# Second-half rows added by the transfer itself: five reads moved from SyncE to GpSimd, tiles finished in the order 3, 0, 2, 1, 4

## The chip, the cores and the metric

The kernel runs on one core of a Trainium2 chip. The metric is the device time of one execution in microseconds (us). Before the change three runs took 617.83, 620.12 and 621.11 us.

## What is computed

The reference is one layer of a flow-matching backbone for 512 latent and 128 context tokens of width 1024: modulation, normalization, attention beside a recurrent block, an output projection with a gated residual, and then a mixture of experts. The change touches only the last line of it, where the experts' output is added to the residual:

```python
x = x + g1 * (jnp.concatenate([attn, rec], axis=-1) @ lp['w_out'])      # x1 of the kernel
h2 = modulate(rms_norm(x, lp['norm2']), sh2, sc2)
x = x + g2 * moe(h2, ...)      # top 1 of 4 groups, then top 2 of its 8 experts
```

Each token has two experts, so each output row is x1 plus two expert rows (already multiplied by g2 and by the expert's weight).

## The kernel before

The 640 tokens are five tiles of 128 rows: tiles 0 to 3 are latent, tile 4 is context. The mixture of experts runs in steps: each takes a pair of experts with up to 64 token slots each, gathers their rows (GpSimd, line 863), multiplies by the weights (TensorE, lines 1821 and 1839), and VectorE (line 1383) evicts the 128 result rows into `y`. GpSimd scatters them to `y_rows` in HBM (line 879), which has 1280 rows: 640 for a token's first expert and 640 for its second. `y_rows` is filled with zeros by ten transfers of GpSimd much earlier (line 842). The rows of the last step are not scattered at all; TensorE multiplies them by a 0/1 matrix `chosen`, which puts each row where its token is, and leaves the result in PSUM. A token's first-half row from the step before the last is sent to the second half, so that the first half can be read one scatter earlier.

The end of the kernel then has, for each tile, four terms: the first-half rows, the second-half rows, x1, and the `chosen` product.

- **SyncE (SP)** waits until all but the last scatter have landed, then issues the loads of the first-half rows into `yk` (line 521: tiles 3, 4, 0, 1, 2) and of the x1 rows of tiles 2, 0 and 1 that had been spilled (line 518, into `x1b`). It then waits for the last scatter (the wait at line 531 ends with it) and issues five loads of the second-half rows into the buffer `y1` (line 533). After that it waits for each finished tile in the order 0 to 4 and issues its store (line 536; tile 4 in two halves, line 540).
- **GpSimd (POOL)** adds x1 to tiles 3 and 4 (line 890), and then the second-half rows to tile 4 (line 893).
- **VectorE (DVE)** adds x1 to tiles 0 and 1 (`base`, line 1395), the first before the eviction of the last step (line 1426), the second after it. It adds the second-half rows to tiles 0, 1 and 2 (`with_late`, line 1402), and to every tile its PSUM sums (`finish`, line 1408; `finish_last` in two halves, line 1416).
- **TensorE (PE)** brings x1 of tile 2 into PSUM with two products by the identity (line 1874), then computes the `chosen` products of the tiles in the order 0 to 4 (line 1889). For tile 3 it also adds the second-half rows by identity products (`PE_SUMS`, line 1887). Tile 4 uses the PSUM bank of tile 0 and waits until that is finished.

Everything in this order is written out by hand with semaphores; `rows_in[t]` counts the transfers that fill tile t (16 each), `y1_in[t]` the second-half transfer, `y_out` the scatters, `fin` the finished tiles. The core of the loop over tiles on VectorE is:

```python
for t in range(3):
    with_late(t)
    finish(t)
dve.wait_ge(S["base"], 1)
finish(3)
dve.wait_ge(S["base"], NT - SPILLED + 1)
finish_last()
```

Of the kernel before, what the change touches and what calls it, by code (L numbers as in the profile page):

```python
# [16 lines left out]
P = 128  # L17
# [7 lines left out]
SPILLED = LT - 1  # L25
PE_SUMS = (3,)
PE_BASE = SPILLED - 1
# [53 lines left out]
def build(nc, a):  # L81

    with ExitStack() as ctx:
# [105 lines left out]
        def temp(c, lo, n):  # L189
# [44 lines left out]
        yk = rf[:, 0:NT * D].rearrange("p (t n) -> p t n", t=NT)  # L234
        y1 = rf[:, NT * D:2 * NT * D].rearrange("p (t n) -> p t n", t=NT)
        x1b = ring[:, HOME[5], 0:SPILLED * D].rearrange("p (t n) -> p t n", t=SPILLED)
# [10 lines left out]
            "out_done v p act xg_in xt_mm gu_mm dn_mm xT_v xT_a th_ok act_ok aT_mm aT_ok y_v idxc_ok pidc_ok y_out "  # L247
            "y_zero gu_half x1b_in base stepw w_mm now gsel chosen tail_mm fin sg_ok turn cache_out st_col st_t st_ev").split()}
        rows_in = [sem(f"rows_in{i}") for i in range(NT)]
# [85 lines left out]
        def tail_bank(t):  # L335

            return (0, 4, 2, 6, 0)[t]

# [27 lines left out]
        def _(sp):  # L366
# [155 lines left out]
            for t in range(SPILLED, NT):  # L522
                first_half(t)
            x1_back(PE_BASE, S["x1b_in"])
            for t in range(PE_BASE):
                x1_back(t, rows_in[t])
                first_half(t)
            first_half(PE_BASE)
            steps = sp.value_load(last[0:1, PAIRS - 1:PAIRS])
            sp.wait_ge(S["y_out"], 16 * steps)  # L530
            sp.sem_inc(S["turn"], 1)
            for t in range(NT):
                sp.dma_start(y1[:, t, :], a["y_rows"][TOK + t * P:TOK + (t + 1) * P, :]).then_inc(y1_in[t], 16)
            for t in range(NT - 1):
                sp.wait_ge(S["fin"], t + 1)
                sp.dma_start(y_dst[t], yk[:, t, :]).then_inc(S["out_done"], 16)
# [267 lines left out]
        def _(pool):  # L804
# [82 lines left out]
            for t in range(SPILLED, NT):  # L887
                pool.wait_ge(rows_in[t], 32)
                row = yk[:, t, :].rearrange("p (c n) -> p c n", c=DC)
                pool.tensor_tensor(row, row, x1_row(t), ALU.add).then_inc(S["base"], 1)  # L890
            pool.wait_ge(S["base"], NT - SPILLED)
            pool.wait_ge(y1_in[NT - 1], 16)
            pool.tensor_tensor(yk[:, NT - 1, :], yk[:, NT - 1, :], y1[:, NT - 1, :], ALU.add).then_inc(S["base"], 1)


        @block.vector
        def _(dve):
# [494 lines left out]
            def base(t):  # L1392

                dve.wait_ge(rows_in[t], 48)
                step(dve.tensor_tensor(yk[:, t, :], yk[:, t, :], x1b[:, t, :], ALU.add))

            def with_late(t):

                if t == PE_BASE:
                    dve.wait_ge(rows_in[t], 32)  # L1400
                dve.wait_ge(y1_in[t], 16)
                step(dve.tensor_tensor(yk[:, t, :], yk[:, t, :], y1[:, t, :], ALU.add))

            def finish(t):

                dve.wait_ge(S["tail_mm"], t + 1)
                b = tail_bank(t)
                dve.tensor_tensor(yk[:, t, :], yk[:, t, :], wide[:, b * 512:b * 512 + D], ALU.add)\
                   .then_inc(S["fin"], 1)
            def finish_last():  # L1410

                b = tail_bank(NT - 1)
                for half in range(2):
                    dve.wait_ge(S["tail_mm"], NT + half)
                    cols = slice(half * 512, (half + 1) * 512)
                    dve.tensor_tensor(yk[:, NT - 1, cols], yk[:, NT - 1, cols], ps[:, b + half, :], ALU.add)\
                       .then_inc(S["fin"], 1)
# [17 lines left out]
            base(1)  # L1435
            for t in range(3):
                with_late(t)
                finish(t)
            dve.wait_ge(S["base"], 1)
            finish(3)  # L1440
            dve.wait_ge(S["base"], NT - SPILLED + 1)
            finish_last()


        @block.tensor
        def _(pe):
# [424 lines left out]
            pe.wait_ge(S["act_ok"], steps * FC + FC)  # L1871
            pe.wait_ge(S["x1b_in"], 16)
            for half in range(2):
# [3 lines left out]
            pe.wait_ge(S["xT_a"], steps + 1)  # L1877
            for t in range(NT):
                if t >= 4:
                    pe.wait_ge(S["fin"], t - 3)  # L1880
                if t in PE_SUMS:
                    pe.wait_ge(y1_in[t], 16)
                for half in range(2):
                    if t == 0:
                        pe.wait_ge(S["y_v"], steps + 1 + half)
                    if t in PE_SUMS:
                        pe.matmul(ps[:, tail_bank(t) + half, :], ident[:, :], y1[:, t, half * 512:(half + 1) * 512],
                                  start=True, stop=False)
                    ins = pe.matmul(ps[:, tail_bank(t) + half, :], chosen[:, t, :],
                                    y[:, half * 512:(half + 1) * 512], start=t not in PE_SUMS and t != PE_BASE, stop=True)  # L1890
                    if half or t == NT - 1:
                        ins.then_inc(S["tail_mm"], 1)
# [60 lines left out]
```

## Time and profile before

| what | us |
|---|---|
| three runs | 617.83, 620.12, 621.11 |
| the profiled execution, own time | 619.67 |
| its span, first to last instruction | 617.8 |
| TensorE busy | 589.3 |
| VectorE busy | 346.2 |
| ScalarE busy | 179.7 |
| GpSimd busy | 102.2 |
| mean granted clock of TensorE, share of full | 0.989 |

The profile is that of one execution. A busy time is the sum of an engine's instructions; a wait is idle time of an engine before an instruction, with what released it. The chain of waits follows the work that ended last back through its releasers. Times in the rows count from the start of the span.

### The profile page before, as it was taken

Reading aid. Unit: us, or ns where it says so; the run is one execution under the profiler, and the core shown is the slowest. Engines: PE = TensorE matmul, PEld = TensorE weight load, DVE = VectorE, ACT = ScalarE, POOL = GpSimd, SP = SyncE. Lnnn points to the kernel's source line nnn. Section 1 sums busy time; section 2 is a strip of 40 time slices with the busy share of each in tenths; the row PEclk is TensorE's granted clock in tenths of the full one; section 3 lists DMA queues with packets and bytes.
Section 4 is the critical chain, followed back from the end, with each engine's and each line's share of the span. In section 5 each row is a group of like instructions: output and inputs, shape, how many; then the busy total and the mean of one; then the engine's idle time right before and its main releaser. Section 6 shows DMA issues by size and latency. Waiting matters only on the chain.

```text
span 617.8 us, 9369 instructions
## 1 busy us (share of the span) xinstructions
PE 589.3 (95%) x3276; PEld 327.9 (53%) x3277; DVE 346.2 (56%) x780; ACT 179.7 (29%) x375; POOL 102.2 (17%) x134
## 2 busy tenths in 40 slices
PE   5989999999998999999999989999999999997997
PEld 2544455455565667645554536555555555554552
DVE  2745898755565888664666784333433343432347
ACT  4203787701145787731111101111111111110110
POOL 4000011121233000000000101212121212121241
PEclk9999999999999999999999889999999999997999
DMA  8999833530028728629113879999999999999997
GB/s 319 375 369 362 321 143 145 188 136 2 1 71 251 301 83 237 285 93 415 71 69 119 310 269 336 415 418 418 420 417 420 417 419 420 419 418 418 419 382 301
DMA packets 47922, 175.95 MB, mean 285 GB/s; under 512 B 11556, under 2 KB 17712, under 8 KB 34320
## 3 DMA queue, kind: packets, MB, share of 16 engines
q1 hardware_dynamic: 36240, 154.60, 64.2%
q0 software_dynamic: 6688, 15.48, 7.2%
q10 hardware_dynamic: 4960, 5.42, 2.5%
q8 instruction: 21, 0.34, 0.2%
q14 instruction: 13, 0.11, 0.0%
HBM read 163.11 MB, written 21.14 MB: 298 GB/s over the span
## 4 chain that ended last, share of the span: by engine, by line
PE 78%; DMA 14%; SPq 4%; DVE 2%; ACTq 1%; issue 1%; ACT 0%; DVEq 0%; POOLq 0%
PE ps L1821 19%; PE ps L1634 11%; PE ps L1839 9%; PE ps L1559 8%; PE ps L1547 7%; DMA expert_w<-exp_w_up 5%; PE ps L1674 4%; PE ps L1701 4%; DMA gate_w<-lru_wx 3%; PE ps L1683 3%; PE ps L1787 2%; DMA w_mod_ring<-w_mod 2%; SPq L374 2%; PE ps L1522 2%; PE ps L1468 2%; DMA recurrence<-w_mod 2%
## 5 line engine op out<-in xcount | busy, mean ns | idle before, releaser
L1821 PE MATMUL ps<-expert_w,hT_mixT 128*64 128x256 f32 x1120 | 136.0, 392 | 6.1 <-DMA expert_w<-exp_w_up 5.7
L1821 PEld LDWEIGHTS ps<-expert_w,hT_mixT 128*64 128x64 f32 x1120 | 84.7, 136 | 61.2 <-issue 17.8
L1547 PE MATMUL ps<-hT_mixT,w 128*128 128x128 f32 (+1 forms) x256 | 72.6, 437 | 1.2 <-DVE hT_mixT L970 1.2
L1634 PE MATMUL ps<-w,hT_mixT 128*128 128x512 f32 x160 | 71.9, 597 | 0.0
L1839 PE MATMUL ps<-expert_w,hT_mixT 128*64 128x512 f32 x276 | 65.8, 598 | 0.0
L786 ACT ACTIVATE hT_mixT<-ps 128x128 f32<-128x128 f32 x36 | 10.0, 278 | 187.1 <-PE ps L1821 187.1
L1547 PEld LDWEIGHTS ps<-hT_mixT,w 128*128 128x128 f32 x256 | 38.9, 191 | 35.8 <-issue 32.6
L1365 DVE SCALAR_TENSOR_TENSOR hT_mixT<-hT_mixT,ps 128x128 f32<-128x128 f32 x36 | 10.4, 288 | 79.8 <-ACT hT_mixT L786 79.8
L1559 PE MATMUL ps<-w_qkv,hT_mixT 128*128 128x512 f32 (+1 forms) x160 | 53.1, 488 | 0.0
L1383 DVE TENSOR_TENSOR w<-ps,w 128x1024 f32<-128x1024 f32 x17 | 20.8, 1225 | 56.6 <-PE ps L1839 56.6
L1634 PEld LDWEIGHTS ps<-w,hT_mixT 128*128 128x128 f32 x160 | 29.1, 191 | 29.9 <-issue 29.7
L1559 PEld LDWEIGHTS ps<-w_qkv,hT_mixT 128*128 128x128 f32 x160 | 29.8, 190 | 21.6 <-issue 19.7
L1839 PEld LDWEIGHTS ps<-expert_w,hT_mixT 128*64 128x64 f32 x276 | 19.0, 136 | 32.3 <-issue 30.3
L1132 DVE TENSOR_REDUCE softmax_stat<-ps 128x1 f32<-128x640 f32 (+1 forms) x40 | 28.6, 715 | 10.3 <-PE ps L1674 10.2
L1674 PE MATMUL ps<-k_stack,q_stack 128*128 128x320 f32 (+1 forms) x144 | 30.6, 331 | 3.3 <-ACT q_work L716 3.3
L879 POOL DMA_INDIRECT y_rows<-w,slot_row_now x17 | 24.0, 1412 | 58.1 <-DVE w L1383 58.1
L1674 PEld LDWEIGHTS ps<-k_stack,q_stack 128*128 128x128 f32 x144 | 21.3, 188 | 16.8 <-issue 11.5
L716 ACT ACTIVATE q_work<-ps,softmax_stat 128x640 f32<-128x640 f32 (+1 forms) x40 | 28.3, 708 | 4.4 <-DVE softmax_stat L1133 3.9
L711 ACT ACTIVATE w_qkv<-ps 128x640 f32<-128x640 f32 (+1 forms) x40 | 24.7, 619 | 14.5 <-PE ps L1683 14.2
L863 POOL DMA_INDIRECT w<-h_rows,slot_token_now x17 | 17.6, 1036 | 66.9 <-PE ps L1787 62.3
L1701 PE MATMUL ps<-w_qkv,v_tok 128*64 128x256 f32 x168 | 25.6, 400 | 0.0
L1683 PE MATMUL ps<-ident,q_work 128*128 128x128 f32 x168 | 25.2, 275 | 0.0
(297 smaller groups left out, 765.5 us busy)
## 6 DMA issues: line engine op xcount, KB each, us to landing
expert_w<-exp_w_down SPq DMA_DIRECT2D x30, 1024.0 KB, 17.5
expert_w<-exp_w_gate SPq DMA_DIRECT2D x29, 1024.0 KB
expert_w<-exp_w_up SPq DMA_DIRECT2D x29, 1024.0 KB
w_mod_ring<-w_mod SPq DMA_DIRECT2D x14, 1024.0 KB, 6.5
y_rows<-zero_rows POOLq DMA_DIRECT2D x10, 512.0 KB, 6.0
expert_w<-y_rows SPq DMA_DIRECT2D x10, 512.0 KB, 7.9
recurrence<-w_mod SPq DMA_DIRECT2D x8, 512.0 KB, 9.8
w<-w_in SPq DMA_DIRECT2D x4, 1024.0 KB, 16.8
```

The lines of the kernel that those rows point to most:

```text
L711: act.activation(probT[:, m % HEADS, 0:k], wide[:, 4 * 512:4 * 512 + k], ACT.Copy).then_inc(S["pT_a"], 1)
L716: act.activation(probs(n), scores(n), ACT.Exp, scale=SCALE, bias=sm[:, 1, n:n + 1], accum_out=sm[:, 2, n:n + 1]).then_inc(S["prob"], 1)
L879: pool.indirect_dma_start(a["y_rows"], bass.IndirectOffsetOnAxis(pidc[:, 0:1], 0), y, None, bounds_check=TOP * TOK - 1, oob_is_err=False). ...
L1132: step(dve.tensor_reduce(sm[:, 0, n:n + 1], scores(n), AXY, ALU.max))
L1547: ins = pe.matmul(ps[:, bank, 0:n], w1v[:, c, m * P:(m + 1) * P], HM[:, c, lo:lo + n], start=(c == 0), stop=(c == DC - 1))
L1559: ins = pe.matmul(ps[:, bank, 0:n], HM[:, c, t * P:(t + 1) * P], wqv[:, c, lo:lo + n], start=(c == 0), stop=(c == DC - 1))
L1634: ins = pe.matmul(ps[:, 2 * (t % 2) + half, :], HM[:, c, t * P:(t + 1) * P], w1v[:, c, half * 512:(half + 1) * 512], start=(c == 0), stop= ...
L1674: ins = pe.matmul(ps[:, bank, 0:k], qs[:, h, t * P:(t + 1) * P], ks[:, g, s, lo:lo + k], start=(s == 0), stop=(s == 1))
L1683: ins = pe.transpose(ps[:, 4 + i // 4, (i % 4) * P:(i % 4 + 1) * P], prob[:, m % 3, i * P:(i + 1) * P], ident[:, :])
L1701: ins = pe.matmul(out.rearrange("p (b n) -> p b n", b=2), vt[:, i if t < LT else NT, g * HD:(g + 1) * HD], probT[:, 4 * g + e:4 * g + 4:2, ...
L1821: ins = pe.matmul(ps[r, 2 + k, 0:2 * P].rearrange("p (k f) -> p k f", k=2), xT[:, c, r], gate_up(i)[:, :, c, k:FF:FC], start=(c == 0), sto ...
L1839: ins = pe.matmul(ps[r, 5 + half, :].rearrange("p (a n) -> p a n", a=4), actT[:, c, r], down(i, c, half), start=(c == 0), stop=(c == FC - 1))
```

## The change

The second-half rows are no longer loaded into a buffer `y1` by SyncE. GpSimd issues five transfers from `y_rows` straight onto `yk` with `accum_op=ALU.add`, so that the transfer adds what it reads to what is there. Each may start only when its tile's first-half rows (and the x1 add, where VectorE or GpSimd makes one) are in `yk`: GpSimd waits for its own two adds, for the last scatter, and between the transfers for VectorE's adds (a new semaphore `own_base`) and for the first-half rows of tile 2. It issues them in the order 3, 0, 4, 2, 1. The adds of the second-half rows on VectorE (three tiles), on GpSimd (tile 4) and on TensorE (tile 3) are gone. TensorE, VectorE and the stores take the tiles in the order 3, 0, 2, 1, 4, with other PSUM banks for them. SyncE goes from its first-half loads straight to the waits for finished tiles.

```diff
--- before.py
+++ after.py
@@ -23,7 +23,7 @@
 NT = TOK // P
 LT = LAT // P
 SPILLED = LT - 1
-PE_SUMS = (3,)
+TAIL = (3, 0, 2, 1, 4)
 PE_BASE = SPILLED - 1
 HEADS, KV, HD = 8, 2, 64
 QK = HEADS + KV
@@ -232,7 +232,6 @@
         th, sg, act2, actT = (HM[:, FC * i:FC * (i + 1), P:2 * P] for i in range(4))
         rf = ring[:, 1:3, :].rearrange("p r n -> p (r n)")
         yk = rf[:, 0:NT * D].rearrange("p (t n) -> p t n", t=NT)
-        y1 = rf[:, NT * D:2 * NT * D].rearrange("p (t n) -> p t n", t=NT)
         x1b = ring[:, HOME[5], 0:SPILLED * D].rearrange("p (t n) -> p t n", t=SPILLED)
         numbers = zero[:, :]
 
@@ -245,7 +244,7 @@
             "mod2_in bc_ok shift_in g2_in route_in prepared bias_mm "
             "pair_ok rank_mm rank_rd slot idx_mm tid_ok gexp_in gexp route_ok "
             "out_done v p act xg_in xt_mm gu_mm dn_mm xT_v xT_a th_ok act_ok aT_mm aT_ok y_v idxc_ok pidc_ok y_out "
-            "y_zero gu_half x1b_in base stepw w_mm now gsel chosen tail_mm fin sg_ok turn cache_out st_col st_t st_ev").split()}
+            "y_zero gu_half base own_base stepw w_mm now gsel chosen tail_mm fin sg_ok turn cache_out st_col st_t st_ev").split()}
         rows_in = [sem(f"rows_in{i}") for i in range(NT)]
         w1_in = [sem(f"w1_in{i}") for i in range(LC)]
         h2_at = [sem(f"h2_at{i}") for i in range(2)]
@@ -334,7 +333,7 @@
 
         def tail_bank(t):
 
-            return (0, 4, 2, 6, 0)[t]
+            return (4, 6, 2, 0, 0)[t]
 
         def at_expert(src, x):
             return src[x] if isinstance(x, int) else src[bass.ds(x, 1)]
@@ -521,18 +520,13 @@
                 sp.dma_start(yk[:, t, :], a["y_rows"][t * P:(t + 1) * P, :]).then_inc(rows_in[t], 16)
             for t in range(SPILLED, NT):
                 first_half(t)
-            x1_back(PE_BASE, S["x1b_in"])
+            x1_back(PE_BASE, x1_at)
             for t in range(PE_BASE):
                 x1_back(t, rows_in[t])
                 first_half(t)
             first_half(PE_BASE)
-            steps = sp.value_load(last[0:1, PAIRS - 1:PAIRS])
-            sp.wait_ge(S["y_out"], 16 * steps)
-            sp.sem_inc(S["turn"], 1)
-            for t in range(NT):
-                sp.dma_start(y1[:, t, :], a["y_rows"][TOK + t * P:TOK + (t + 1) * P, :]).then_inc(y1_in[t], 16)
-            for t in range(NT - 1):
-                sp.wait_ge(S["fin"], t + 1)
+            for i, t in enumerate(TAIL[:-1]):
+                sp.wait_ge(S["fin"], i + 1)
                 sp.dma_start(y_dst[t], yk[:, t, :]).then_inc(S["out_done"], 16)
             for half in range(2):
                 sp.wait_ge(S["fin"], NT + half)
@@ -888,9 +882,19 @@
                 pool.wait_ge(rows_in[t], 32)
                 row = yk[:, t, :].rearrange("p (c n) -> p c n", c=DC)
                 pool.tensor_tensor(row, row, x1_row(t), ALU.add).then_inc(S["base"], 1)
+            def second_half(t):
+                pool.dma_start(yk[:, t, :], a["y_rows"][TOK + t * P:TOK + (t + 1) * P, :], accum_op=ALU.add).then_inc(y1_in[t], 16)
             pool.wait_ge(S["base"], NT - SPILLED)
-            pool.wait_ge(y1_in[NT - 1], 16)
-            pool.tensor_tensor(yk[:, NT - 1, :], yk[:, NT - 1, :], y1[:, NT - 1, :], ALU.add).then_inc(S["base"], 1)
+            pool.wait_ge(S["y_out"], 16 * (end + 1))
+            pool.sem_inc(S["turn"], 1)
+            second_half(3)
+            pool.wait_ge(S["own_base"], 1)
+            second_half(0)
+            second_half(4)
+            pool.wait_ge(rows_in[PE_BASE], 32)
+            second_half(2)
+            pool.wait_ge(S["own_base"], 2)
+            second_half(1)
 
 
         @block.vector
@@ -1392,24 +1396,19 @@
             def base(t):
 
                 dve.wait_ge(rows_in[t], 48)
-                step(dve.tensor_tensor(yk[:, t, :], yk[:, t, :], x1b[:, t, :], ALU.add))
-
-            def with_late(t):
-
-                if t == PE_BASE:
-                    dve.wait_ge(rows_in[t], 32)
+                dve.tensor_tensor(yk[:, t, :], yk[:, t, :], x1b[:, t, :], ALU.add).then_inc(S["own_base"], 1)
+
+            def finish(i, t):
+
                 dve.wait_ge(y1_in[t], 16)
-                step(dve.tensor_tensor(yk[:, t, :], yk[:, t, :], y1[:, t, :], ALU.add))
-
-            def finish(t):
-
-                dve.wait_ge(S["tail_mm"], t + 1)
+                dve.wait_ge(S["tail_mm"], i + 1)
                 b = tail_bank(t)
                 dve.tensor_tensor(yk[:, t, :], yk[:, t, :], wide[:, b * 512:b * 512 + D], ALU.add)\
                    .then_inc(S["fin"], 1)
             def finish_last():
 
                 b = tail_bank(NT - 1)
+                dve.wait_ge(y1_in[NT - 1], 16)
                 for half in range(2):
                     dve.wait_ge(S["tail_mm"], NT + half)
                     cols = slice(half * 512, (half + 1) * 512)
@@ -1433,12 +1432,8 @@
             base(0)
             last_y_evict(end)
             base(1)
-            for t in range(3):
-                with_late(t)
-                finish(t)
-            dve.wait_ge(S["base"], 1)
-            finish(3)
-            dve.wait_ge(S["base"], NT - SPILLED + 1)
+            for i, t in enumerate(TAIL[:-1]):
+                finish(i, t)
             finish_last()
 
 
@@ -1869,25 +1864,20 @@
                 visits(q, q % HELD, 1 + q // HELD, kept=q == PAIRS - 2, kept_half=q == KEPT_HALF)
             steps = pe.value_load(last[0:1, PAIRS - 1:PAIRS])
             pe.wait_ge(S["act_ok"], steps * FC + FC)
-            pe.wait_ge(S["x1b_in"], 16)
+            pe.wait_ge(x1_at, 16 * (SPILLED + 1))
             for half in range(2):
                 pe.matmul(ps[:, tail_bank(PE_BASE) + half, :], ident[:, :], x1b[:, PE_BASE, half * 512:(half + 1) * 512],
                           start=True, stop=False)
             pe.wait_ge(S["chosen"], NT)
             pe.wait_ge(S["xT_a"], steps + 1)
-            for t in range(NT):
-                if t >= 4:
-                    pe.wait_ge(S["fin"], t - 3)
-                if t in PE_SUMS:
-                    pe.wait_ge(y1_in[t], 16)
+            for i, t in enumerate(TAIL):
+                if i == NT - 1:
+                    pe.wait_ge(S["fin"], 1)
                 for half in range(2):
-                    if t == 0:
+                    if i == 0:
                         pe.wait_ge(S["y_v"], steps + 1 + half)
-                    if t in PE_SUMS:
-                        pe.matmul(ps[:, tail_bank(t) + half, :], ident[:, :], y1[:, t, half * 512:(half + 1) * 512],
-                                  start=True, stop=False)
                     ins = pe.matmul(ps[:, tail_bank(t) + half, :], chosen[:, t, :],
-                                    y[:, half * 512:(half + 1) * 512], start=t not in PE_SUMS and t != PE_BASE, stop=True)
+                                    y[:, half * 512:(half + 1) * 512], start=t != PE_BASE, stop=True)
                     if half or t == NT - 1:
                         ins.then_inc(S["tail_mm"], 1)
```

## Rows read from the trace of the kernel before

**Rows 1.** The page: busy time by engine; shares of the chain by engine.

```profile
PE 589.3 (95%) x3276; PEld 327.9 (53%) x3277; DVE 346.2 (56%) x780; ACT 179.7 (29%) x375; POOL 102.2 (17%) x134
...
PE 78%; DMA 14%; SPq 4%; DVE 2%; ACTq 1%; issue 1%; ACT 0%; DVEq 0%; POOLq 0%
```

**Rows 2.** Chain of waits, 590 to 618 us: start us, us, what.

```profile
601.24 1.91 PE ps L1874 x4
603.15 5.15 PE ps L1889 x12
608.30 1.12 PE ps L1887 x2
609.42 0.86 PE ps L1889 x2
610.28 0.86 PE ps L1887 x2
611.14 0.87 PE ps L1889 x2
```

**Rows 3.** Instructions of VectorE in order of time, 590 to 618 us: start us, us.

```profile
599.09 1.23 DVE L1395 TENSOR_TENSOR expert_w<-expert_w 128x1024 f32<-128x1024 f32 x1 [1.82 <-DMA expert_w<-y_rows]
...
602.72 1.22 DVE L1395 TENSOR_TENSOR expert_w<-expert_w 128x1024 f32<-128x1024 f32 x1
604.24 1.23 DVE L1402 TENSOR_TENSOR expert_w<-expert_w 128x1024 f32<-128x1024 f32 x1 [0.30 <-DMA expert_w<-y_rows]
605.50 1.22 DVE L1408 TENSOR_TENSOR expert_w<-expert_w,ps 128x1024 f32<-128x1024 f32 x1
...
610.28 1.22 DVE L1408 TENSOR_TENSOR expert_w<-expert_w,ps 128x1024 f32<-128x1024 f32 x1
612.11 1.22 DVE L1408 TENSOR_TENSOR expert_w<-expert_w,ps 128x1024 f32<-128x1024 f32 x1 [0.61 <-PE ps L1889]
613.25 1.28 DVE L1416 TENSOR_TENSOR expert_w<-expert_w,ps 128x512 f32<-128x512 f32 x2
```

**Rows 4.** Issues on SP's queue in order of time, 560 to 618 us.

```profile
587.45 0.80 SPq L521 DMA_DIRECT2D expert_w<-y_rows  x2
...
590.99 0.94 SPq L521 DMA_DIRECT2D expert_w<-y_rows  x2
599.09 2.29 SPq L533 DMA_DIRECT2D expert_w<-y_rows  x5
606.75 6.94 SPq L536 DMA_DIRECT2D y_sample<-expert_w  x4
```

**Rows 5.** Instructions of GpSimd in order of time, 560 to 618 us.

```profile
595.86 2.38 POOL L890 TENSOR_TENSOR expert_w<-expert_w,x_tok 128x1024 f32<-128x1024 f32 x1
609.65 2.81 POOL L893 TENSOR_TENSOR expert_w<-expert_w 128x1024 f32<-128x1024 f32 x1 [11.42 <-DMA expert_w<-y_rows]
```

**Rows 6.** Windows of 2 us: last columns are TensorE's clock, DMA busy share, GB/s.

```profile
599.00:601.00 2.00, 2.00 (x12) 0.50 (x8) 1.23 (x1) 0.00 (x0) 0.00 (x0) 1.00 1.02 393
...
605.00:607.00 2.00, 2.00 (x6) 0.91 (x5) 1.97 (x3) 0.00 (x0) 0.00 (x0) 1.00 1.06 418
```

**Rows 7.** DMA by queue, 599 to 609.6 us: packets, MB, share.

```profile
q1 hardware_dynamic: 1048, 3.79, 92.2%
```

**Rows 8.** Zero-filling transfers issued by GpSimd (line 842), and their order of time.

```profile
L842 POOL DMA_DIRECT2D y_rows<-zero_rows x10: 847/976/1167, 180.1 to 211.2; - x10
...
DMA to landing us min/median/max: 3.9/6.0/11.8
...
188.41 2.60 POOL L842 DMA_DIRECT2D y_rows<-zero_rows  x3 [5.61 <-issue]
197.12 2.81 POOL L842 DMA_DIRECT2D y_rows<-zero_rows  x3 [6.11 <-issue]
211.18 1.00 POOL L842 DMA_DIRECT2D y_rows<-zero_rows  x1 [11.25 <-issue]
```

**Rows 9.** The first-half loads (line 521): issue to landing.

```profile
DMA to landing us min/median/max: 5.9/10.2/11.4
```

## The prediction

> **What bounds the kernel now.** I went from the page to the end of the kernel. The page shows TensorE busy for 95% of the span and on the chain of waits for most of it [rows 1]; but the change leaves the expert loop alone and touches only what follows the last expert step, so the question is which wait ends last between about 599 us and the end. The chain of waits there [rows 2] is TensorE's: the identity products that put the x1 rows of tile 2 into PSUM, then the `chosen` products of tiles 0, 1 and 2 without a gap (5.15 us, 1.72 a tile), then tile 3, which needs 3.7 us as it also adds its second-half rows by two identity products (1.12 and 0.86), then tile 4. VectorE adds tile 3, then the two halves of tile 4, and the queue stores them. VectorE itself [rows 3] is the second chain: from 604.24 it is full with three pairs of adds of 1.22 us and ends them at 611.50, 0.6 us before TensorE lets it go on with tile 3. Its last add ends at 613.25 + 1.28 = 614.53; 3.3 us later the span of 617.8 ends.
>
> The third party is the transfers. The first-half rows and the x1 rows go out on SP's queue from 587.45 on, and after the last scatter but one has landed (599.09) the five second-half loads follow within 2.3 us [rows 4]. They land late and one by one: VectorE gets tile 0 at 604.24 [rows 3], TensorE waits for tile 3 until 608.30 [rows 2], GpSimd for tile 4 until 609.65 [rows 5]. From the first to the fifth that is 5.4 us, 1.35 us a tile of 512 KB, about 390 GB/s, and the windows show why: the 16 DMA engines are full until 607, at 393 GB/s in the first window and 418 in the last [rows 6]. Until 609.6 SP's queue moved 3.79 MB [rows 7]; less five loads (2.62) and the store of tile 0 (0.52), 0.65 MB were still left of the first-half rows at 599.1, 1.7 us of work. So the landings follow a simple sum: 599.1 + 1.7 + 2.0 (issue and landing) + 1.35 for each tile, which gives 604.15 for the first and 609.55 for the fifth, against 604.24 and 609.65 in the trace.
>
> **Part by part.** *Removed from VectorE:* three adds of second-half rows, 3 x 1.22 = 3.7 us [rows 3]. *From TensorE:* two identity products for tile 3 (1.12 + 0.86) and the wait in front of them; five tiles then take 5 x 1.72 from 603.15, that is until 611.7, where they now end at 613.7. *From GpSimd:* the add of tile 4, 2.81 us [rows 5], which ends at 612.5 and is covered by TensorE now. *From SP:* the wait for the scatter and five issues (2.29 us), which nothing else was waiting behind: its stores start at 606.75.
>
> *With the transfers free of charge* the end would go by TensorE and VectorE: four adds end at 610.0 + 0.1 + 1.22 = 611.4, the halves of tile 4 at about 612.6, 1.9 us before 614.53. That is the most this change can gain, 0.3% of the run. A measurement of this kernel tells about 0.5% (3.1 us) from no change.
>
> *Moved to GpSimd:* five transfers. GpSimd is done with its two base adds at 598.24 [rows 5], before the scatter lands at 599.09, so moving that wait costs nothing. An issue on GpSimd takes 0.98 us where SP takes 0.46, 2.29 for five [rows 4, 8]: the first transfer starts 0.5 us later, the others wait in the DMA queue in any case. The order is tile 3 (599.1), the wait for VectorE's base add of tile 0 (ends 600.3 [rows 3]), tiles 0 and 4 (until 602.3), the wait for the first-half rows of tile 2, tile 2 (about 603.3), and the wait for VectorE's base add of tile 1, which runs behind the last eviction and ends at 603.94; tile 1 is issued until 604.9. Behind each wait stand all later transfers, and VectorE's finishing adds wait for them. The first-half rows of tile 2 were issued last, at about 591.5; such loads land 5.9 to 11.4 us after issue [rows 9], so by 602.9 at the latest. With the engines busy on the earlier tiles, none of these waits empties the queue.
>
> *The unknown price* is that of a transfer that adds; no row shows one. For each 512 KB it has to read the row in HBM and also the row that is in `yk`, and to write once. Call s the time of one tile. Not under 1.35, since it reads all that the plain load reads and the engines are full with those; the nearest row for moving both operands is two plain transfers, 2 x 1.35 = 2.7. With reads, reads and write one after another it would be three, 4.05. I take 2.7: the windows show 1.0 busy share at the rate of one read and one write [rows 6], so nothing is free there for a second read. The Trainium skill, "Collectives: The Full Stack", section "The bandwidth ceiling", says that a reducing step runs at about half the rate of a copying one, since both operands are read through the same ring; no run of before shows it, and by it the sum would be the one below. The Trainium skill, "DMA: Bandwidth & Descriptors", section "Anatomy of one DMA", gives for a transfer from GpSimd 2.0 us plus its bytes at 436 GB/s and no surcharge for an add, 1.2 us a tile as an estimate; by it the change would come out as the first rival.
>
> **The sum.** Landings, from 599.1 + 1.7 + 2.0 = 602.8: tile 3 at 605.5, tile 0 at 608.2, tile 4 at 610.9, tile 2 at 613.6, tile 1 at 616.3. VectorE: tile 3 605.6 to 606.8, tile 0 608.3 to 609.5, then it idles until 613.7, tile 2 until 614.9, tile 1 616.4 to 617.6, the halves of tile 4 until 618.9. Against 614.53 that is +4.4 us. The last stores leave with the same spacing as now, so the 3.3 us behind them stay. In general the end moves by 5s - 9.1 us, and never below -1.9: no change at s = 1.8, +0.5% at s = 2.45. The stores of tiles 3 and 0 now leave at 606.8 and 609.5, amid the transfers; at 1.35 each that is up to 2.7 more, +7.1 in all. Now the store of tile 0, issued at 606.75, runs amid the loads of tiles 3 and 4 without widening the 1.35, so I count nothing for it and keep +7.1 as the upper end. The profiled execution took 619.67 us, 1.9 around its span of 617.8, and with +4.4 would be 624.1; the median of the runs, 620.12, is 0.45 higher, and the forecast is for it: 624.5.
>
> **The rivals.** *Adding costs no more than loading (s = 1.35).* Tile 3 lands at 604.7 for the slower issue, tile 0 at 606.0, tile 4 at 607.4, tile 2 at 608.7, tile 1 at 610.1; VectorE ends tile 3 at 606.2, tile 0 at 607.9, tile 2 at 610.0, tile 1 at 611.4, the halves at 612.7: -1.8, 618.3 us. For it: the second operand is on the chip already, and only the read from HBM may count. Against it: full engines at one read per byte. It decides below s = 1.8. Chance 0.24.
> *In between (s from 1.7 to 2.4),* if the second read goes on in part beside the write: -0.6 to +2.9, at s = 2.0 +0.9, 621.0. Chance 0.17.
> *Room in GpSimd's queue.* The zero-filling transfers of the same size, also issued by GpSimd, went out three at a time, with 5.6, 6.1 and 11.3 us of idling in between which no instruction explains [rows 8]. If adding transfers need as much room, tiles 3, 0 and 4 go out until 602.3, then GpSimd stands 5.6 to 11.3 us; tile 1 is out at about 609.9 at the earliest and lands 3.9 later (the fastest landing there [rows 8]), 613.8; then adds of 1.3 and 1.28 until 616.4: +1.9, up to +7.6 with the long stall, even at s = 1.35. Against it: those transfers read their zeros in pieces of 512 bytes, these read whole rows of 4 KB. Chance 0.07, mostly slower.
> *Three times the cost (s = 4.05):* +11, 631. Chance 0.07.
> The forecast, s of about 2.5 to 3 with or without the stores' share (+3.3 to +7.1): chance 0.45; its own range is 623.4 to 627.2.
>
> **How the numbers follow.** Faster by over 0.5% is in none of these cases: 0.02 for what I have not seen. Within 0.5%: the cheap case less that 0.02, the one in between, and 0.02 of the queue's: 0.41. Slower: 0.45 + 0.05 + 0.07 = 0.57. The range runs from the cheap case, 618.0, to a little over the upper end with both stores, 628.0; the tripled cost and the long stall lie outside.
>
> **What would show it.** The time from the issue of an adding transfer to VectorE's finishing add, and the spacing of the finishes of tiles 0, 2 and 1: 5.4 and 2.7 us by the forecast, with VectorE waiting for GpSimd's transfers about 4 us before tile 2 and 1.5 before tile 1; by the cheap case it waits for TensorE and is never idle over 1 us. TensorE should end its products at 611.7 in either, and GpSimd issue five transfers between 599 and 605; a gap after the third is the queue's room. I am wrong if VectorE's last add ends before 617 with 2.7 a tile, or if the time before 599 us moves by over 1 us.

## The result, and the profile after

Seven runs of the changed kernel took 622.72 to 626.54 us, median 624.29; seven of the kernel before, taken beside them, took 617.83 to 621.11, median 619.60. The ratio is 1.0095 (5.9 us), 95% interval 1.0075 to 1.0114: slower by 4.6 to 7.1 us; the two medians are 4.7 apart. The profiled execution has a span of 623.4 us against 617.8.

The page of the changed kernel: span, busy times, and the chain's shares by engine (as in [rows 1]).

```profile
span 623.4 us, 9352 instructions
...
PE 585.7 (94%) x3272; PEld 326.4 (52%) x3273; DVE 343.2 (55%) x777; ACT 179.7 (29%) x375; POOL 103.2 (17%) x138
...
PE 73%; DMA 17%; SPq 4%; DVE 2%; issue 1%; ACTq 1%; ACT 0%; DVEq 0%; POOL 0%; POOLq 0%
```

TensorE has 3.6 us less to do, VectorE 3.0, and TensorE's share of the chain has gone from 78 to 73%, that of the transfers from 14 to 17. The chain of waits at the end (start, duration, what) says where, against [rows 2]:

```profile
589.82 12.38 DMA expert_w<-y_rows
...
603.04 14.70 DMA expert_w<-y_rows
...
617.76 0.04 DVE expert_w L1406
...
617.91 1.66 DVEq L83
619.58 0.60 DVE expert_w L1415
```

TensorE isn't in it any more. It runs from the first-half rows over GpSimd's last issue to 14.7 us of waiting for one transfer, the second-half rows of tile 1, and from there to VectorE. VectorE in order of time, against [rows 3]:

```profile
598.44 1.22 DVE L1399 TENSOR_TENSOR expert_w<-expert_w 128x1024 f32<-128x1024 f32 x1 [2.45 <-DMA expert_w<-y_rows]
...
601.38 1.21 DVE L1399 TENSOR_TENSOR expert_w<-expert_w 128x1024 f32<-128x1024 f32 x1
604.60 1.22 DVE L1406 TENSOR_TENSOR expert_w<-expert_w,ps 128x1024 f32<-128x1024 f32 x1 [2.01 <-DMA expert_w<-y_rows]
607.65 1.22 DVE L1406 TENSOR_TENSOR expert_w<-expert_w,ps 128x1024 f32<-128x1024 f32 x1 [1.84 <-DMA expert_w<-y_rows]
614.33 1.22 DVE L1406 TENSOR_TENSOR expert_w<-expert_w,ps 128x1024 f32<-128x1024 f32 x1 [5.45 <-DMA expert_w<-y_rows]
617.76 1.22 DVE L1406 TENSOR_TENSOR expert_w<-expert_w,ps 128x1024 f32<-128x1024 f32 x1 [2.21 <-DMA expert_w<-y_rows]
618.90 1.28 DVE L1415 TENSOR_TENSOR expert_w<-expert_w,ps 128x512 f32<-128x512 f32 x2
```

The four lines 1406 are the finishes of tiles 3, 0, 2 and 1. Before each VectorE sat idle until its adding transfer landed: 2.01, 1.84, 5.45 and 2.21 us. TensorE had ended its `chosen` products long before, at 601.71 + 8.75 = 610.46:

```profile
601.71 8.75 PE L1879 MATMUL ps<-w,hT_mixT 128*128 128x512 f32 x20
```

GpSimd (against [rows 5]) waits for the last scatter, for VectorE and for the first-half rows of tile 2, 2.1 us in all, and has issued everything by 604.24:

```profile
595.20 2.37 POOL L884 TENSOR_TENSOR expert_w<-expert_w,x_tok 128x1024 f32<-128x1024 f32 x1
598.45 1.00 POOL L886 DMA_DIRECT2D expert_w<-y_rows  x1 [0.88 <-DMA y_rows<-w,slot_row_now]
599.97 1.84 POOL L886 DMA_DIRECT2D expert_w<-y_rows  x2 [0.52 <-DVE expert_w L1399]
602.48 1.76 POOL L886 DMA_DIRECT2D expert_w<-y_rows  x2 [0.67 <-DMA expert_w<-y_rows]
```

The windows of the transfers in that time show full engines, as [rows 6], but half the bytes: 205 and 211 GB/s at a share over 1.0 (each added row is counted once). The stores join them late: the one of tile 3 is issued at 605.84, but SyncE's queue q1 moves nothing from 603 to 609 and 0.73 MB from 609 to 615, with the adding transfers (q0) beside it. The second fence gives the two queues for 609 to 615.

```profile
603.00:605.00 2.00, 2.00 (x6) 0.95 (x5) 0.40 (x1) 0.00 (x0) 1.24 (x2) 1.00 1.07 205
...
607.00:609.00 2.00, 2.00 (x6) 0.81 (x5) 1.22 (x1) 0.00 (x0) 0.00 (x0) 1.00 1.07 211
...
611.00:613.00 2.00, 0.00 (x0) 0.00 (x0) 0.00 (x0) 0.00 (x0) 0.00 (x0) 1.00 1.05 281
```

```profile
q0 software_dynamic: 234, 0.88, 73.8%
q1 hardware_dynamic: 195, 0.73, 32.4%
```

The queues from 598 to 618 us (packets, MB, share of 16 engines) price it: GpSimd's queue, q0, moved its five tiles with 69.0% of 20 us, 2.76 us a tile. This share runs a little high for adding transfers, since their packets overlap (the share of the windows above is 1.07).

```profile
q0 software_dynamic: 720, 2.62, 69.0%
q1 hardware_dynamic: 655, 2.36, 29.9%
```

Counted from TensorE's first `chosen` product (602.99 before, 601.71 after), VectorE's last add ends after 11.5 us before and after 18.5 us now; the expert loop ended 1.3 us earlier in this profiled execution, so the span shows 5.6 of the 6.9.

### The profile page after: what moved, and what is told of

It reads as the page before. It is cut to its first block, busy times and chain, and to the rows that moved or that the text cites. A ratio compares the mean times of both kernels' runs of the same rounds, so it can differ in the third digit from the quotient of the medians.

```text
span 623.4 us, 9352 instructions
## 1 busy us (share of the span) xinstructions
PE 585.7 (94%) x3272; PEld 326.4 (52%) x3273; DVE 343.2 (55%) x777; ACT 179.7 (29%) x375; POOL 103.2 (17%) x138
## 4 chain that ended last, share of the span: by engine, by line
PE 73%; DMA 17%; SPq 4%; DVE 2%; issue 1%; ACTq 1%; ACT 0%; DVEq 0%; POOL 0%; POOLq 0%
PE ps L1816 17%; PE ps L1629 11%; PE ps L1542 8%; PE ps L1554 8%; PE ps L1834 7%; DMA expert_w<-exp_w_up 5%; DMA expert_w<-y_rows 4%; PE ps L1669 4%; PE ps L1696 4%; DMA gate_w<-lru_wx 3%; PE ps L1517 3%; PE ps L1678 3%; SPq L373 2%; PE ps L1463 2%; PE ps L1782 2%; DMA recurrence<-w_mod 2%
## 5 line engine op out<-in xcount | busy, mean ns | idle before, releaser
L1387 DVE TENSOR_TENSOR w<-ps,w 128x1024 f32<-128x1024 f32 x17 | 20.8, 1224 | 56.5 <-PE ps L1834 56.5
L1669 PEld LDWEIGHTS ps<-k_stack,q_stack 128*128 128x128 f32 x144 | 21.3, 188 | 17.2 <-issue 11.5
```

Source lines behind the costliest of these rows:

```text
L1669: ins = pe.matmul(ps[:, bank, 0:k], qs[:, h, t * P:(t + 1) * P], ks[:, g, s, lo:lo + k], start=(s == 0), stop=(s == 1))
```

## Experiments

All runs below start from one of the two kernels. They also bound each step number that an engine loads, with two register instructions per load; a control with that alone was not run. Kernels with and without the adding have it alike. The time behind "beside" is the median of the kernel before in the same rounds, and the ratio has its 95% interval in brackets. In what follows "first issue" is the issue of the first second-half transfer, 599.09 in the kernel before and 598.45 in the changed one, where the last add ends 21.7 us later (15.4 in the kernel before). What released that issue differs between the runs, so the count from TensorE's first `chosen` product (18.5 and 11.5 us) stands beside it where the two disagree.

**Plain transfers in the same places.**

```diff
-pool.dma_start(yk[:, t, :], ..., accum_op=ALU.add).then_inc(y1_in[t], 16)
+pool.dma_start(yk[:, t, :], ...).then_inc(y1_in[t], 16)
```

> The changed kernel with the adding taken off its five transfers: GpSimd issues the same reads at the same places, onto the same rows, but they overwrite what is there (so the first-half rows and the x1 added to them are left out of the output). As in all runs that follow, the step numbers that the engines load are bounded by two more register instructions each; that is before the stage in question, so times of the stage are counted from the landing of the last scatter. Theory (an adding transfer takes 2.6 to 2.7 us of the full engines where a plain one takes 1.35): the five take 1.35 each, VectorE's last add ends some 5 to 7 us earlier than in the changed kernel, counted from the landing of the last scatter; the time is 618 to 619.5 us, 0 to 2 below the kernel before. Rival 1 (issuing from GpSimd, or its waits, is what costs): the time stays near 624, and the gap between the issue and the landing stays at 6 to 15 us. Rival 2 (the order of the tiles costs): VectorE still waits over 4 us before tile 2.

618.61 us (10 runs) beside 618.14; ratio 1.001 (0.9995 to 1.0025). VectorE (order of time) now waits 1.3 us or less before a finish, and q0 (20 us again) needs 37.3%, 1.49 us a tile:

```profile
604.26 2.49 DVE L1406 TENSOR_TENSOR expert_w<-expert_w,ps 128x1024 f32<-128x1024 f32 x2 [1.32 <-DMA expert_w<-y_rows]
608.08 1.22 DVE L1406 TENSOR_TENSOR expert_w<-expert_w,ps 128x1024 f32<-128x1024 f32 x1 [1.32 <-DMA expert_w<-y_rows]
610.18 1.22 DVE L1406 TENSOR_TENSOR expert_w<-expert_w,ps 128x1024 f32<-128x1024 f32 x1 [0.89 <-DMA expert_w<-y_rows]
611.32 1.28 DVE L1415 TENSOR_TENSOR expert_w<-expert_w,ps 128x512 f32<-128x512 f32 x2
```

```profile
q0 software_dynamic: 720, 2.62, 37.3%
```

The last add ends 612.60 - 598.94 = 13.7 us after the first issue, 8 us sooner than with the adding; from TensorE's first product it is 11.0 us, 7.5 sooner. The order, the waits and GpSimd as the issuer are all still there, so the loss is the adding's. The bounds on the step numbers are not behind it: two kernels below have them together with the adding, and take 624.17 and 625.18 us. The gain of 1.8 us that the cheap case promised did not show in the time. In the profile the last add is 1.7 us sooner than in the kernel before by the first issue, but only 0.6 by TensorE's first product, and the stores behind it took 4.2 us where they had taken 3.3. GpSimd stood 1.16 and 1.45 us between its issues, and the engines were only 0.69 busy from 599 to 601; how much of the gain that cost was not separated.

**GpSimd as the issuer, nothing else.** The kernel before, its five plain loads into `y1` moved from SyncE to GpSimd, behind the two base adds.

```diff
-sp.wait_ge(S["y_out"], 16 * steps)
-...
-for t in range(NT):
-    sp.dma_start(y1[:, t, :], a["y_rows"][...]).then_inc(y1_in[t], 16)
...
 pool.wait_ge(S["base"], NT - SPILLED)
+pool.wait_ge(S["y_out"], 16 * (end + 1))
+...
+for t in range(NT):
+    pool.dma_start(y1[:, t, :], a["y_rows"][...]).then_inc(y1_in[t], 16)
```

> The kernel before with its five plain second-half loads issued by GpSimd, behind its two base adds and its own wait for the last scatter, in place of SyncE. Nothing else is changed. Theory (who issues a transfer is worth less than a microsecond, the adding is what costs): the first load starts 0 to 0.5 us later, they take 1.35 to 1.5 us a tile, and the time is that of the kernel before within 1 us. Rival (transfers through GpSimd's queue are slow by themselves): 2 us a tile or more, and the time rises by 3 us or more.

619.33 us (9 runs) beside 618.57; ratio 1.0027 (1.001 to 1.0044). The five loads cost 33.8% of 20 us, 1.35 a tile, as SyncE's did. In the profile the last add ends 15.2 us after the first issue, as before (15.4). By the interval this kernel is 0.6 to 2.7 us slower, which may be more than the 1 us expected, but is not 5. How much of it is GpSimd's issuing and how much the bounds was not separated; four other kernels with the same bounds lie within 0.1% of the kernel before (ratios 0.9992 to 1.001).

```profile
q0 software_dynamic: 722, 2.62, 33.8%
```

This run also has loads and stores in different queues, which the kernel before has not. The first store is issued at 606.83. From 603 to 607 only the loads' queue q0 moves anything (1.65 MB). The stores' queue q1 starts after 607, when 0.27 MB of the loads are left:

```profile
q1 hardware_dynamic: 122, 0.47, 57.7%
q0 software_dynamic: 83, 0.27, 33.1%
```

**Half the columns.**

```diff
-pool.dma_start(yk[:, t, :], a["y_rows"][...], accum_op=ALU.add).then_inc(...)
+pool.dma_start(yk[:, t, 0:D // 2], a["y_rows"][..., 0:D // 2], accum_op=ALU.add).then_inc(...)
```

> The changed kernel with adding transfers of 512 of the 1024 columns (the right halves of the second-half rows are left out of the output); rows of 2 KB in place of 4 KB, as many rows. Theory (both operands are read, so the cost goes by bytes): the five adding transfers take 1.3 to 1.5 us of the 16 engines each, by their queue's share and by the spacing of the finishes, as full plain ones do, and VectorE's last add ends 13 to 15 us after the first issue, against 21.7 in the changed kernel and 13.7 with plain transfers; 618 to 620 us. Rival (a fixed cost of each added row, or of each transfer): the spacing stays above 2.2 us a tile, the last add comes over 18 us after the first issue, and the time is above 622.

618.32 us (10 runs) beside 618.81; ratio 0.9992 (0.9975 to 1.0009). The queue moved 1.31 MB with 39.5%, 1.58 us a tile, against 2.76 for 2.62 MB. That is a little over the 1.3 to 1.5 expected. If the cost is a part per transfer and a part by bytes, the two numbers give 0.4 and 2.36 us for a full tile: it goes mostly by bytes. A price that goes mainly by rows is out, as the packets are as many (720). The end is TensorE's again for three finishes of four (the releasers say so), and the last add comes 13.0 us after the first issue. The spacing of these finishes is therefore TensorE's and says nothing on the transfers.

```profile
q0 software_dynamic: 720, 1.31, 39.5%
```

```profile
604.07 1.22 DVE L1406 TENSOR_TENSOR expert_w<-expert_w,ps 128x1024 f32<-128x1024 f32 x1 [1.11 <-PE ps L1879]
605.78 1.22 DVE L1406 TENSOR_TENSOR expert_w<-expert_w,ps 128x1024 f32<-128x1024 f32 x1 [0.49 <-PE ps L1879]
607.71 1.22 DVE L1406 TENSOR_TENSOR expert_w<-expert_w,ps 128x1024 f32<-128x1024 f32 x1 [0.70 <-DMA expert_w<-y_rows]
609.22 1.22 DVE L1406 TENSOR_TENSOR expert_w<-expert_w,ps 128x1024 f32<-128x1024 f32 x1 [0.29 <-PE ps L1879]
```

**No store before the last landing.**

```diff
+for t in range(NT):
+    sp.wait_ge(y1_in[t], 16)
 for i, t in enumerate(TAIL[:-1]):
```

> The changed kernel, where SyncE starts no store before all five adding transfers have landed. Theory (the stores of tiles 3 and 0 take engine time from the adding transfers of tiles 2 and 1, 1.35 us each): VectorE's finish of tile 2 and that of tile 1 come 2 to 3 us earlier, counted from the first issue; the distance from the finish of tile 0 to that of tile 2 falls from 6.7 to about 5.4 us; but the stores then leave at the end, 2.6 MB at 390 GB/s are 6.7 us plus 2, so the kernel ends 0 to 3 us later than the changed one. Rival (stores run in gaps that the adding transfers leave, the spacing is their own): the spacing stays at 6.5 to 6.9 us, and the time rises by 3 to 5.

625.18 us (4 runs) beside 618.81; ratio 1.0112 (1.0077 to 1.0148), which overlaps that of the changed kernel. The finishes:

```profile
605.01 1.22 DVE L1408 TENSOR_TENSOR expert_w<-expert_w,ps 128x1024 f32<-128x1024 f32 x1 [2.42 <-DMA expert_w<-y_rows]
607.48 1.22 DVE L1408 TENSOR_TENSOR expert_w<-expert_w,ps 128x1024 f32<-128x1024 f32 x1 [1.25 <-DMA expert_w<-y_rows]
612.50 1.22 DVE L1408 TENSOR_TENSOR expert_w<-expert_w,ps 128x1024 f32<-128x1024 f32 x1 [3.80 <-DMA expert_w<-y_rows]
614.96 1.22 DVE L1408 TENSOR_TENSOR expert_w<-expert_w,ps 128x1024 f32<-128x1024 f32 x1 [1.24 <-DMA expert_w<-y_rows]
```

With the stores out of the way the adding transfers land at a steady 2.5 us: 2.47 from tile 3 to tile 0, 5.02 for two tiles to tile 2, 2.46 to tile 1. The last add ends 19.0 us after the first issue, 2.7 sooner than in the changed kernel, as two stores at 1.35 would have it; from the finish of tile 0 to that of tile 1, the stretch in which stores ran, it is 2.6 sooner (7.48 against 10.11). The split is not as clean as that: by the landing of tile 1 in the changed kernel, at 617.7, SyncE's queue had moved 1.54 MB since 609, nearly three stores, and the last 0.05 MB of the adding transfers went out among them after 615. Then all stores run at the end and it takes 5.9 us to the end of the span where it had been 3.2. So the stores do take time from the adding transfers, and their total must be moved in any case. By the queue's share a tile costs 2.72 us here (68.1% of 20 us), nearly the 2.76 of the changed kernel: 2.5 and 2.7 are two readings of one price, by spacing and by share.

**The order of issue 3, 0, 2, 1, 4.**

```diff
 second_half(0)
-second_half(4)
 ...
 second_half(1)
+second_half(4)
```

> The changed kernel with its transfers issued in the order in which the tiles are finished: 3, 0, 2, 1, 4 in place of 3, 0, 4, 2, 1. Theory (one queue of 2.6 to 2.7 us a tile that ends at the same moment whatever the order): tile 2 and tile 1 land one tile time earlier, tile 4 last, at the moment where tile 1 lands now; VectorE then has only the two halves of tile 4 left, so its last add ends 1.2 us earlier, 20.5 us after the first issue against 21.7, and the time falls by about 1 us. Rival (waits at GpSimd set the landings): the wait for the first-half rows of tile 2 now stands in front of the third transfer, the queue runs empty, and the gain is under 0.3 us.

624.17 us (6 runs) beside 618.81; ratio 1.0086 (1.0056 to 1.0116), not to be told from 1.0095. The gain of 1.2 us that the theory has isn't shown: the last add comes 20.8 us after the first issue in place of 21.7, but 18.1 after TensorE's first product in place of 18.5. The wait of the theory has moved as said, with 2.62 us now before the halves of tile 4. The rival's wait is there too: GpSimd stood 1.43 us for the first-half rows of tile 2 before its third transfer, and the engines were 0.69 busy from 599 to 601.

```profile
610.63 1.22 DVE L1406 TENSOR_TENSOR expert_w<-expert_w,ps 128x1024 f32<-128x1024 f32 x1 [1.65 <-DMA expert_w<-y_rows]
614.43 1.22 DVE L1406 TENSOR_TENSOR expert_w<-expert_w,ps 128x1024 f32<-128x1024 f32 x1 [2.57 <-DMA expert_w<-y_rows]
618.26 1.28 DVE L1415 TENSOR_TENSOR expert_w<-expert_w,ps 128x512 f32<-128x512 f32 x2 [2.62 <-DMA expert_w<-y_rows]
```

**One adding transfer in the kernel before, for tile 4.** It is issued when the rows of tile 0 have landed, in place of that tile's load and of GpSimd's add.

```diff
-pool.wait_ge(y1_in[NT - 1], 16)
-pool.tensor_tensor(yk[:, NT - 1, :], yk[:, NT - 1, :], y1[:, NT - 1, :], ALU.add)
+...                                        # its own wait for the last scatter
+pool.wait_ge(y1_in[0], 16)
+pool.dma_start(yk[:, NT - 1, :], a["y_rows"][...], accum_op=ALU.add).then_inc(y1_in[NT - 1], 16)
```

> The kernel before with one adding transfer, that of tile 4, issued by GpSimd when the second-half rows of tile 0 have landed, in place of its plain load and of GpSimd's add of 2.81 us; the other four loads, VectorE's and TensorE's sums and the order 0 to 4 are those of before. Theory (an adding transfer costs 1.35 us more of the engines' time and is harmful only where they are full and something waits for it): it lands at about 611 to 612, before TensorE's last products at 613.7, and the time is that of the kernel before within 1 us. Rival (adding transfers disturb the others, or a GpSimd-issued one lands 8 us or more after its issue whatever the load): VectorE's last halves start after 614.5, and the time rises by 1 us or more.

619.13 us (12 runs) beside 618.81; ratio 1.0005 (0.999 to 1.002). It is issued at 604.91 and lands 5.9 us later, at 610.8, while TensorE still has products to do until 613.9. The same operation that costs some 5 us five times over costs nothing that can be measured here (the interval is -0.6 to +1.2 us). It is no cheaper in itself: its queue took 14.8% of 20 us, 3.0 us of the engines. But these were 0.71 busy from 605 to 607, and nothing waited for it. (TensorE began 1.1 us earlier in this profile and then waited 1.24 us for the plain load of tile 3.)

```profile
L895 POOL DMA_DIRECT2D expert_w<-y_rows x1: 991/991/991, 604.9 to 604.9; - x1
...
DMA to landing us min/median/max: 5.9/5.9/5.9
```

**Two kernels built to win.** Both finish the tiles in the order 0, 1, 3, 2, 4, take the second-half products off TensorE and give tiles 3 and 4 to GpSimd's adds. In the first, tile 2 gets its rows by an adding transfer, in the second VectorE adds them after a plain load.

```diff
+TAIL = (0, 1, 3, 2, 4)
-PE_SUMS = (3,)
...
 # GpSimd, behind its base adds
+...                                        # first kernel only, down to the transfer
+pool.wait_ge(rows_in[PE_BASE], 32)
+pool.dma_start(yk[:, PE_BASE, :], a["y_rows"][...], accum_op=ALU.add).then_inc(y1_in[PE_BASE], 16)
+for t in range(SPILLED, NT):
+    pool.wait_ge(y1_in[t], 16)
+    pool.tensor_tensor(yk[:, t, :], yk[:, t, :], y1[:, t, :], ALU.add).then_inc(S["base"], 1)
```

> Built from the kernel before: tiles finished in the order 0, 1, 3, 2, 4; plain loads by SyncE for tiles 0, 1, 3 and 4; GpSimd adds the second-half rows of tiles 3 and 4 (two adds of 2.8 us), TensorE has no second-half products left, VectorE adds those of tiles 0 and 1 only, and tile 2 gets them by one adding transfer. Theory (an adding transfer takes 2.5 us alone, and a store in its way 1.35): TensorE ends its products at 611.7, but tile 2 lands at 599.1 + 1.7 + 2.0 + 4 x 1.35 + 2.5 + 1.35 = 612.0, counted with the scatter landing at 599.1; VectorE's last add ends at 614 to 614.5, no more than 0.5 us before that of the kernel before; same time within 0.3%. Rival (the adding transfer runs beside the others at little cost): tile 2 lands by 610, the last add ends at 612.8 to 613.3, and the time falls by 1 to 1.7 us.

> The same without any adding transfer: tile 2 is loaded by SyncE between tiles 3 and 4 and VectorE adds it. Theory: VectorE is full from 604.3 with three late adds, four finishes and the two halves, 9.8 us, and ends at about 614.1, 0.4 us before the kernel before and level with or before the kernel that has one adding transfer; same time within 0.3%. Rival (the plain loads land too late for that order): VectorE waits over 1 us in between and its last add ends after 615.

The first took 618.65 us (11 runs) beside 618.57, ratio 1.0004 (0.9992 to 1.0016); the second 619.65 (10 runs), ratio 1.0026 (1.0016 to 1.0037). Neither beats the kernel before. In both profiles the last scatter landed over 4 us earlier (the loads are issued at 594.87 and 594.32), so my absolute times for them do not apply. Counted from TensorE's first `chosen` product the last add ends after 12.2 and 13.3 us, where the kernel before has 11.5. In the first, tile 2 landed 7.1 us after its issue, at 609.4, and is not what VectorE waits for. VectorE waits 0.99 us there for GpSimd, whose two adds take 5.63 us. In the second VectorE is full. One of its adds beside GpSimd's took 2.13 us where it takes 1.22 alone, though others beside them took 1.22; GpSimd's two took 6.55, where a single one took 2.81 in the kernel before. How far the bounds on the step numbers have a part in the 0.26% stays open.

```profile
605.36 6.55 POOL L894 TENSOR_TENSOR expert_w<-expert_w 128x1024 f32<-128x1024 f32 x2 [8.65 <-DMA expert_w<-y_rows]
```

```profile
606.43 1.22 DVE L1407 TENSOR_TENSOR expert_w<-expert_w,ps 128x1024 f32<-128x1024 f32 x1
607.57 2.13 DVE L1401 TENSOR_TENSOR expert_w<-expert_w 128x1024 f32<-128x1024 f32 x1
```

## Why the prediction was right, point by point

*The unknown price,* s = 2.7 us a tile for the adding transfer against 1.35 for a plain one: 2.5 by the spacing with no store beside, 2.76 by the queue's share; plain in the same place 1.49, and 1.35 from GpSimd's hands in the kernel before. The 2.5 lies at the low end of the forecast's 2.5 to 3 and just above the case in between, which went to 2.4. The reason given for it, that full engines have nothing free for a second operand, is borne out as far as the windows go (share over 1.0 at 205 GB/s) and by the half width: the cost goes mostly with the bytes. Whether the second read or the adder itself sets the pace was not separated; both would go by bytes. That full engines aren't needed for it is shown by the single transfer, which cost as much engine time (3.0 us) where they had room. By the Trainium skill's rule on reducing steps ("Collectives: The Full Stack", "The bandwidth ceiling"), about half a copy's rate, the measured 205 against 393 to 418 GB/s agrees. By the Trainium skill's formula for a transfer from GpSimd ("DMA: Bandwidth & Descriptors", "Anatomy of one DMA") a tile would cost 1.2 us as an estimate, which holds roughly for the plain ones (1.35 to 1.49) and not for the adding ones.

*The stores' share* is the term that was mis-sized. I counted nothing for the stores of tiles 3 and 0 and kept +2.7 as the upper end, since the store of tile 0 had not widened the spacing of the plain loads. That reading was wrong: the store was hardly among them. Where the two can be told apart (GpSimd as the issuer) the stores' queue moves its first bytes after 607, with 0.27 MB of the loads left. The adding transfers were still running when the stores came in after 609, and there they cost: from the finish of tile 0 to that of tile 2 it took 6.7 us, not 5.4, and from there to tile 1 3.4, not 2.7; holding the stores back gave back 2.7. It was offset in part by s being 2.5 and not 2.7 (1.0 over five tiles). VectorE's last add, counted from TensorE's first `chosen` product, moved by 6.9 us, near the upper end of +7.1 and not at +4.4. The median of all runs moved by 4.7, the ratio of the runs says 5.9 (4.6 to 7.1). So the range and the mechanism were right, but that the forecast 624.5 lies 0.2 us from the 624.29 measured is luck: it took +4.4 without the stores' cost, and added it to a median of three runs, 620.12, that was 0.5 us above the median of seven.

*The other parts* came as costed. TensorE ended its products 8.75 us after the first, as the sum had it (five tiles of 1.72). GpSimd issued five transfers between 598.45 and 604.24. VectorE waited 5.45 us before tile 2 and 2.21 before tile 1, where I had said about 4 and 1.5. One sign that I had named as against me did occur: the time before 599 us moved by 1.3 us, the last scatter being issued at 590.02 in place of 591.30. The runs above, with the same loop, issue it between 586.9 and 590.8, four of them built from the kernel before, so the change need not be its cause. The one profile of the kernel before is the latest of the ten.

*The rivals.* The cheap add is out: the plain transfers show what it would have given, and the adding ones cost nearly twice that. Room in GpSimd's queue is out: after the third issue it stood 0.67 us, and the profile names the first-half rows of tile 2 as the releaser. The tripled cost is out. The order of the transfers, which I had not priced, is worth 0.3 or 0.9 us in the profiles, by the two counts, and nothing that the times can tell.

## What to carry to other kernels

A transfer that adds saves an engine's add and a buffer, but costs the DMA engines nearly twice a plain one. Price it against what waits: here 3 x 1.22 us of VectorE and 2 us of TensorE were exchanged for 5 x 1.2 to 1.4 us of engines that were full, with a queue of landings that the end waited for; a single one, placed where the engines had room and nothing waited, cost nothing measurable. And when the transfers last until the stores come in, stores that used to be free begin to count.

## What the runs showed that was not expected

- GpSimd needs longer to issue an adding transfer: 0.87 to 1.26 us each (up to 1.56 in the kernel with the other order of issue), against about 0.55 for the same transfer without the adding.
- A store's bytes move well after its issue while another queue keeps the engines full: none in the 3.2 us from 605.84 to 609 beside the adding transfers. Whether stores beside plain loads would cost as much isn't shown, since the loads were nearly done when the stores came in.
- In the last stage the landing of the plain loads depended little on when they were issued: with the issue at 596.77 (the kernel with one adding transfer) tile 0 still landed at 604.70, as with 599.09 (604.24), probably since the first-half rows are in front of it.
- TensorE's granted clock was 0.53 from 613 to 615 us and 0.50, the lower of its two levels (1.2 GHz), from there on in the changed kernel, after its products had ended at 610.46. Nothing followed on TensorE, so it cost nothing: the lower mean clock of that run (0.984 against 0.989) is no cause of the loss.
